# Second transformer block regrouped by tiles 0-1, 2, 3 (early part) and 0-2, 3 (conv FFN), with expert rows spaced wider

## What is computed

```python
# first block
x = x + (sigmoid(gc) * short_conv + sigmoid(ga) * diff_attention) @ w_mix_out
x = x + cross_attention(rmsnorm(x), rmsnorm(mem))
x = x + peer_ffn(rmsnorm(x))          # 8 heads x 16 of 16384 experts per token
x = rmsnorm(x)
# second block
y = concat(rms(nsa_mixer(...)), rms(gmlp_mixer(zg)), rms(conformer_conv(zc, 31 taps)))
x = x + y @ w_out
x = x + memory_cross_attention(x, mem_2)
x = x + conv_ffn(x)                   # up 1024->5632, conv of 3 taps over tokens, silu gate, down 2816->1024
out = rmsnorm(x)
# peer_ffn, per token: act = gelu(h . u_e);  out = sum_e g_e * act * v_e
```

## Time and profile before

| | before |
|---|---|
| median of 3 runs | 2905.69 us (2903.39 to 2906.92) |
| the profiled execution | 2902.87 us, span 2901.1 us, mean granted clock 0.892 |
| TensorE busy | 2408.7 us (83%) |
| VectorE busy | 1765.4 us (61%) |
| ScalarE busy | 1124.4 us (39%) |
| DMA | 838.74 MB, mean 289 GB/s |
| expert gathers (GpSimd queue) | 512, 536.90 MB, first at 557.1 us, last at 2267.5 us |

### The profile page before, as it was taken

The page is one execution under the profiler, slowest core; times in us unless marked ns, Lnnn a source line. Parts: engine busy times, 40 slices in busy tenths (PEclk is TensorE's granted clock), DMA queues, the critical chain, the costliest instruction groups (busy, mean ns, idle before and its releaser), DMA issues.

```text
span 2901.1 us, 31007 instructions
## 1 busy us (share of the span) xinstructions
PE 2408.7 (83%) x10834; PEld 1655.5 (57%) x10834; DVE 1765.4 (61%) x4230; ACT 1124.4 (39%) x2762; POOL 665.2 (23%) x569
## 2 busy tenths in 40 slices
PE   8999999879978649778958588577984799988998
PEld 7786666657744327536626434354762376655873
DVE  2101311598797778676999898888998417312430
ACT  2101311242533764354442578464554225412210
POOL 0000000122343344332233334443234102100000
PEclk9999999989989879999979566699996699999999
DMA  6555343589999999999889989999999653443443
GB/s 205 173 153 166 96 145 126 213 333 371 403 412 417 416 392 391 419 398 393 314 333 416 368 324 379 390 419 419 416 418 419 258 161 111 152 131 94 153 153 116
DMA packets 160972, 838.74 MB, mean 289 GB/s; under 512 B 17400, under 2 KB 21896, under 8 KB 95024
## 3 DMA queue, kind: packets, MB, share of 16 engines
q0 software_dynamic: 73728, 536.90, 45.8%
q1 hardware_dynamic: 82464, 287.75, 28.6%
q10 hardware_dynamic: 4624, 12.11, 1.2%
HBM read 828.27 MB, written 8.41 MB: 288 GB/s over the span
## 4 chain that ended last, share of the span: by engine, by line
PE 50%; DVE 22%; ACT 13%; DMA 10%; issue 4%; POOL 0%; ACTq 0%; DVEq 0%; SPq 0%
PE ps L909 24%; DMA BIG<-in_uv,BIG 9%; DVE BIG L1951 6%; PE ps L929 5%; DVE X L1928 5%; PE ps L930 5%; PE ps L1153 5%; PE ps L910 3%; ACT L1446 2%; PE ps L1180 2%; DVE BIG L1859 1%; DVE BIG L1856 1%; PE ps L1123 1%; PE ps L1102 1%; ACT WK L1228 1%
## 5 line engine op out<-in xcount | busy, mean ns | idle before, releaser
L2168 POOL DMA_INDIRECT BIG<-in_uv,BIG x512 | 622.0, 1215 | 1635.1 <-DVE X L1928 576.0
L909 PE MATMUL ps<-BIG,RING 128*128 128x256 f32 x3472 | 810.6, 386 | 15.2 <-DMA RING<-in_w_cq 4.9
L909 PEld LDWEIGHTS ps<-BIG,RING 128*128 128x128 f32 x3472 | 665.5, 193 | 148.0 <-issue 26.5
L1951 DVE CUSTOM_DVE_ANT_0 BIG<-BIG 128x1024 f32<-128x1024 f32 x512 | 619.2, 1217 | 87.1 <-DMA BIG<-in_uv,BIG 84.8
L1928 DVE SCALAR_TENSOR_TENSOR X<-BIG,small,X 128x1024 f32<-128x1024 f32 x333 | 426.3, 1280 | 75.0 <-ACT small L1450 74.3
L1446 ACT ACTIVATE small<-small 128x1 f32<-128x1 f32 x512 | 102.7, 201 | 640.5 <-DVE small L1951 636.3
L909 PE MATMUL ps<-WK,RING 128*128 128x256 f32 x1232 | 291.0, 389 | 21.3 <-DVE BIG L1707 19.3
L909 PEld LDWEIGHTS ps<-WK,RING 128*128 128x128 f32 x1232 | 238.6, 195 | 62.2 <-DVE BIG L1707 26.8
L929 PE MATMUL ps<-RING,BIG 128*128 128x512 f32 (+1 forms) x448 | 225.7, 585 | 5.6 <-DVE BIG L1686 2.4
L930 PE MATMUL ps<-RING,BIG 128*128 128x512 f32 (+1 forms) x448 | 223.5, 580 | 0.0
L1279 ACT ACTIVATE BIG<-ps 128x256 f32<-128x256 f32 (+2 forms) x143 | 56.5, 397 | 375.8 <-PE ps L910 316.7
(11 more groups left out here) (258 smaller groups left out, 2860.1 us busy)
## 6 DMA issues: line engine op xcount, KB each, us to landing
RING<-in_w_up SPq DMA_DIRECT2D x88, 512.0 KB
RING<-in_w_down SPq DMA_DIRECT2D x66, 512.0 KB
RING<-in_w_pq SPq DMA_DIRECT2D x32, 512.0 KB
RING<-in_w_cc SPq DMA_DIRECT2D x16, 512.0 KB
RING<-in_w_cx SPq DMA_DIRECT2D x16, 512.0 KB
RING<-in_w_cb SPq DMA_DIRECT2D x16, 512.0 KB
RING<-in_w_cv SPq DMA_DIRECT2D x16, 512.0 KB
RING<-in_w_gc SPq DMA_DIRECT2D x16, 512.0 KB
```

The costliest lines, as they stand in the source:

```text
L909: e.matmul(ps[:, 0:256], W[:, j, :], src[:, j, 0:256], start=j == 0, stop=False)
L1951: e.tensor_tensor_reduce(out=u, in0=HF[:, t % 2, :], in1=u, scale=1.0, scalar=0.0, op0=ALU.mult, op1=ALU.add, accum_out=dots[:, k % 8:k % ...
L2168: e.indirect_dma_start(out=slot[i], out_offset=None, in_=I["uv"], in_offset=bass.IndirectOffsetOnAxis(ap=IDX[:, t, c:c + 1], axis=0)).then ...
```

## The change

- The second block's early part (`second(g)`, up to `xo`) runs for three groups, tiles 0-1, tile 2 and tile 3 (`EARLY`), its conv FFN (`ffn(f)`) for tiles 0-2 and tile 3 (`LATE`).
- `work` now has `second(0)`, then, once `total(2)` is placed and all choices are made, `second(1)` (tile 2) and `ffn(0)` (tiles 0-2, `up` with 384 columns a chunk). The part after the weave (`end`) is `second(2)` and `ffn(1)` for tile 3, with `late_down` for three tiles (66 chunks) beside, then `down` of tile 3.
- `beside` takes two or three chunks after each attention step, 8 at `y`, 6 in the norm ahead of `xq`, one after each cross attention step, and the rest in the norm ahead of `up`.
- A `proj_T` chunk costs the planner 1.7 per tile. An expert costs 3.1, 3.1, 3.2, 3.4 for tiles 0 to 3.
- Seven slots from the scores of half 1 to the end (slot 7 holds part of the FFN's activations). `UPT`, the buffers of the up half, are two for tiles 0-2 and four for tile 3.
- Tables, loads and loops are indexed by group; `final_in`, the layer-norm row and the compressed values are loaded once per group, and the eight attention units of tile 2 are scaled on ScalarE, where those of tiles 2-3 had one of two wide scalings on GpSimd (line 2147).

```diff
+EARLY = ((0, 1), (2,), (3,))
+LATE = ((0, 1, 2), (3,))
+def tiles_of(name, h):
+    if name in EARLY_SITES or name in ("mix2", "y", "fa"):
+        return EARLY[h]
+    if name in ("up", "ffn2", "fb", "down"):
+        return LATE[h]
+    return (2 * h, 2 * h + 1) if h < 2 else (0, 1)
...
-        if i >= (8 if self.lent_from is None or (3, 3) in self.chosen else 7):
+        if i >= (8 if self.lent_from is None else 7):
...
-                yield 3.4, "proj_T", site, h, c, m, k
+                yield 1.7 * len(tiles_of(site, h)), "proj_T", site, h, c, m, k
...
+        n = 2 if layer == 1 else len(EARLY[h])
+        for step in self.phase(True, ((4.0, "cross", layer, h, i, lean) for i in range(4 * n + 4))):
+            yield step
+            yield from beside(1)
...
-        for i in range(2):
+        for i in LATE[0]:
             for f in range(22):
                 k = self.next_ring()
                 yield (0, "chunk", "down", f, k), (1.7, "down", 0, f, k, (i,))
...
-        for step in self.phase(True, ((8.0, "nsa", h, i) for i in range(20))):
+        for step in self.phase(True, ((8.0, "nsa", h, i) for i in range(8 * nt + 4))):
...
-            yield from beside(1 + step[3] % 2)
+            yield from beside(2 + step[3] % 2)
...
+    def ffn(self, f, lean, beside=lambda n: ()):
+        yield 0, "mark", ("f", f)
+        yield from self.norm_steps(("ffn2", f), lean)
+        yield from beside(100)
+        for k in range(8):
+            yield (3.0 if k == 7 else 0), "trans", ("ffn2", f), k, lean
+        self.norming = False
+        yield 0, "mark", ("up", f)
+        for step in self.proj_T("up", f, 11, lean):
+            yield step
+            if f and step[1:] == ("out_T", "up", f, 1, 3, lean):
+                yield from self.last(0)
...
+        yield from self.second(2, False, beside)
+        yield from self.ffn(1, False, beside)
+        for f in range(22):
+            k = self.next_ring()
+            yield 0, "chunk", "down", f, k
+            yield 3.4, "down", 1, f, k, (0,)
+        yield 0, "mark", ("out", 1)
+        yield from self.last(1)
...
         yield from self.second(0, True)
+        while ("total", 2) not in self.reached or (3, 3) not in self.chosen:
+            self.light = True
+            yield "wait"
+        self.light = False
+        yield from self.second(1, True)
+        yield from self.ffn(0, True)
         self.light = True
...
-                yield (3.1 if t < 2 else 2.5), "pace"
+                yield (3.1, 3.1, 3.2, 3.4)[t], "pace"
...
-        yield from (s[1:] for s in self.second(1, False))
+        yield from (s[1:] for s in self.end())
...
+                n = 128 * len(tiles_of(site, h))
                 for j in range(7):
-                    e.matmul(ps[:, 0:256], W[:, j, :], src[:, j, 0:256], start=j == 0, stop=False)
+                    e.matmul(ps[:, 0:n], W[:, j, :], src[:, j, 0:n], start=j == 0, stop=False)
...
-                if h == 1 and 0 <= u < 16:
+                if h == 2 and 0 <= u < len(nsa_units(h)):
```

More of the change, by code:

```diff
@@ L325, in late_down, with second @@
         yield (0, "mark", ("out", 0)),
[L327 to L332, removed]
+    def second(self, h, lean, beside=lambda n: ()):
+        nt = len(EARLY[h])
         yield 0, "mark", ("s2", h)
@@ L376, in second @@
         yield 0, "y_scale", h
-        yield from beside(7)
+        yield from beside(8)
         for k in range(8):
@@ L381, in second @@
         yield from self.proj_tok("ou", h, 2, lean)
[L382 to L395, removed]
+        yield from self.cross(2, h, lean, beside)
+    def ffn(self, f, lean, beside=lambda n: ()):
+        yield 0, "mark", ("f", f)
+        yield from self.norm_steps(("ffn2", f), lean)
+        yield from beside(100)
+        for k in range(8):
+            yield (3.0 if k == 7 else 0), "trans", ("ffn2", f), k, lean
+        self.norming = False
+        yield 0, "mark", ("up", f)
[3 more added lines that the diff above has]
+                yield from self.last(0)
     def last(self, h):
@@ L400, in last, with end, beside @@
         yield 0, "store", h
+    def end(self):
+        rest = self.late_down()
+        def beside(n):
+            for steps in islice(rest, n):
+                yield from steps
+        yield from self.second(2, False, beside)
[6 more added lines that the diff above has]
+        yield from self.last(1)
     def first_a(self):
@@ L464, in peers @@
                     yield 0, "total", t - 1
-                yield (3.1 if t < 2 else 2.5), "pace"
+                    self.reached.add(("total", t - 1))
+                yield (3.1, 3.1, 3.2, 3.4)[t], "pace"
             if t % 2:
@@ L611, in program @@
[L611 to L619 removed]
+        L = [L0, L0, SLOT0 + 8448]
@@ new lines, in program, with early @@
+        NT = [len(g) for g in EARLY]
+        def early(first, *shape):
+            return [at_(o + first * n, *[128 * n if d == "w" else n if d == "n" else d for d in shape]) for o, n in zip(L, NT)]
+        QN = early(0, 4, "w")
+        ZG = early(512, "n", 512)
+        CV = early(1024, 2, "w")
+        ZT = early(1280, 2, "w")
+        Y = early(1536, "n", 1024)
+        HTz = early(1536, 8, "w")
+        YT = early(0, 8, "w")
+        HTx = early(2048, 8, "w")
+        QT2 = early(0, 8, "w")
@@ L1411, in cross @@
                             w.wait_ge(*at["mm", "xv", layer, h, hd, d])
-                            e.activation(OT[:, 2 * hd + d, :], banks[ps_of["xv", layer, h, hd, d]][:, 0:256], ACT.Copy,
+                            e.activation(OT[:, 2 * hd + d, :], banks[ps_of["xv", layer, h, hd, d]][:, 0:128 * nt], ACT.Copy,
                                          scale=1.0).then_inc(act.sem, act("ev", "xv", layer, h, hd, d))
@@ L2161, in expert @@
                     w.wait_ge(*at["sum", slot_before[k]])
-                    if i == NS - 1 and slot_before[k] == plan.lent_from:
-                        w.wait_ge(*at["idx", 3, 3])
                 else:
@@ L2200, in gpsimd_program @@
                             channel_multiplier=-1).then_inc(pool.sem, pool("ws"))
-            follow({"norm_out": norm_out, "nsa": nsa, "out_T": out_T, "expert": expert, "mark": marks(pool, "pool")})
+            follow({"nsa": nsa, "out_T": out_T, "expert": expert, "mark": marks(pool, "pool")})
         for engine_program in (tensor_program, vector_program, scalar_program, gpsimd_program, sync_program):
```

341 lines of the change are left out of this document (183 added, 158 removed).

## The result

| | before | after |
|---|---|---|
| median | 2905.62 us (2899.99 to 2914.76) | 2913.01 us (2906.92 to 2915.69) |
| ratio | | 1.0023, 95% interval 1.0016 to 1.003 |
| span of the profiled execution | 2901.1 us | 2910.0 us |
| `second(0)`, to PE's last record of `xo` (1482 to 1991.6; 1479.5 to 1939.1) | 509.6 us, 164 dots | 459.6 us, 130 dots |
| last dot of an expert | 2283 | 2400 |

A forecast was written before the change was run, and what follows sets the result against it. DVE was taken to bound 1482:1823 and DMA the rest to 2283, with PE busy 578 of the tail's 618 us. Last dot at 2365, plus 74 for remaining `up` chunks and 386 of tail, gave 2825, rounded to 2828 us; range 2785 to 2885.

The forecast's parts named there:

- One tile halves: Tail of tile 3: 128 moving columns take about 0.11 us a record, a one-tile weight chunk of 16 records 1.72 us.
- Rival 4: Tail: 128-row weight loads don't run under 128-column multiplies, 0.214 us a record; +110 us, 2938 us; chance 0.03.
- Rival 1: Tail: SP's queue starves the ring at 226 GB/s, 2.32 us a one-tile chunk; +64 us, 2892 us; chance 0.10.
- Rival 2: Weave: seven slots instead of eight allow only 3.93 us an expert; +106 us, 2934 us; chance 0.08.
- Rival 3: Weave: the plan's unit costs 1.25 us, not the expert; last dot at 2538, about 3000 us; chance 0.07, mostly in part.
- Rival 5: Weave: better balance, DVE and DMA reach 94%, last dot near 2330; 2790 us; chance 0.10.
- sign of being wrong: The prediction is wrong if the experts' last dot comes after 2440 or the tail exceeds 450 us.
- 33.5 for 42 saves 8.7 x 2.58: Norm, projections and compression of tiles 0-1: 33.5 experts instead of 42 at 2.58 us each save 22 us of 148.
- 45 for 58 in the DMA-bound stage saves 12.6 x 2.51: `ou` to `xo` of tiles 0-1: 45 experts instead of 58 at 2.51 us of DMA each save 32 us of 175.
- my step to 432 for the totals by DVE and by bytes: Tile 2's experts: stages sum to 440 us; totals give 434 by DVE, 424 by bytes; 432 was taken.
- PE can be some five chunks ahead: After the last expert: 19 `up` chunks of three tiles remain, but PE's lead leaves 14 or 15, 74 us.
- `last(0)` in it costs about 10 us of DVE and ScalarE, which eight banks cover: `up` of tile 3: `last(0)` hides under eight banks (13.8 us); without that cover it costs up to 10 us.

The follow-up runs named there:

- e1: Changed kernel with only the store of tiles 0-2's output placed 12 chunks later in `up` of tile 3; 2896.98 us, 0.9968 of before.
- e3: Changed kernel with the eighth slot given back to the experts after the last choice; 2915.14 us, 1.0028 of before.
- e2: Changed kernel with the old expert spacing of 2.5 units for tiles 2 and 3, so regrouping alone; 2999.77 us, 1.0319 of before.
- e5: Changed kernel with the store 12 chunks later and tile 3's experts at 4.8 units ahead of `up`, 3.4 beside it; 2853.65 us, 0.9817 of before.

## Why the prediction was wrong

**Right.** The plan's stages: `second(0)` took all of tile 2's experts, tile 3's ended after 24 chunks of `up` (forecast 25), some 20 were left (19), and a chunk of 384 columns took 5.16 us (5.13). The tail without its stall: 391 us in e1 for 386. One tile halves: 128 records of 128 columns ran in 14.5 us (2765.9 to 2780.4), 0.113 us each, where I had 0.107 to 0.11. The norm, projections and compression of tile 2 took 97.4 us for 92, and its `y` to `up` 121.8 for 121, with DMA full in both. Rival 4 is out. The sentence of the Trainium skill that stood beside it (TensorE: Matmul & The Clock Gate, The mechanism; I had named the section behind it), by which weight loads overlap multiplies in flight only when they use other row groups, does not hold for this shape. The same section also has loads pulled ahead when they go to the background weight buffer; whether that is what happened, no run here shows. Rival 1 is out: the ring gave a one-tile `up` chunk every 1.79 us, PE's own pace. Rival 2 is out by e3. Rival 3 was wrong in size, 1.09 us a unit and not 1.25, but right that the work beside has a cost of its own. Rival 5 (last dot near 2330) is out too. Neither sign of being wrong came (last dot after 2440, tail over 450): the miss is four terms of 16 to 27 us that all went the same way.

**The first failed step, +22 and +16: "33.5 for 42 saves 8.7 x 2.58" and its two neighbours.** I priced each expert that leaves a stage at the full time of the resource that looked busiest, 2.5 to 2.6 us (1.8 in the attention), and so took DVE or DMA for a hard bound in every stage. Between PE's marks `second(0)` gave back 50 us for 34.5 experts, 1.45 us each. Worst was "45 for 58 in the DMA-bound stage saves 12.6 x 2.51": `y` to `xo` gave back 4 us for 9 experts, and at the changed kernel's density neither half the bytes (0 us) nor the shorter sums (0.5 us) made it shorter; PE is busy 127 us of its 148. The share of 1.01 in the earlier trace rows did not make the DMA the bound there. Norm to compression gave 2.1 us an expert and not 2.58. The attention gave more than I took, 28 us for 22, because 17 experts left it and not 12. The cuts of the earlier trace rows, put where the plan has its stages, lay up to 17 us beside PE's (its attention ended at 1840 and not 1823, its `up` ran from 2011 to 2196 and not from 1998 to 2208), which hid this. My three terms came to 76 us, to 440; the remaining 8 us of the +22 are my step to 432 for the totals by DVE and by bytes, which price in the same way.

The forecast for the early part of tile 2, 310 us, was a sum of each stage's largest resource at full use. Up to `up` it took 340: +12 ahead of the attention (6 of them `xo` of tiles 0-1, still running), +13 in the attention (115 us for 102, DVE busy 99 of them and the DMA share 0.75), +1 behind it, and +6 for the six ring buffers whose lead I had taken off. The experts' part of `up` then took 127 for 141, which leaves the +16.

**The second, +27: "PE can be some five chunks ahead".** That took the state of 1998:2208, where PE waited, over to a stage where PE bounds: beside the 35 experts PE did its 24 to 25 chunks of 5.16 us without a pause and was never ahead. My own two terms, 141 + 74 = 215 us for all 44 chunks, lay below the 44 x 5.13 = 226 that PE needs. Adding them up would have shown it. (That 1.5 x 3.45 is 5.18 and not 5.13 adds 2 us at most.) The gap of those two terms is 12 us of the 27; the other 15 are only the last dot coming earlier in `up` than forecast, and stand with the other sign in the 127 for 141.

**The third, +23: "`last(0)` in it costs about 10 us of DVE and ScalarE, which eight banks cover".** The cover was right for these two engines. Missing was the store at the end of `last(0)`: I had written that SP's ring order follows PE's, and had not counted the one other instruction that `last` puts on that queue. It cost 18.3 us of the 23 in the traces (97.2 against 78.9 for `up`) and 16 in the medians; the few left are spread over the tail.

**What the change is worth.** The tail became 208.5 us shorter. What lies ahead of it became 220 us longer: tile 2's early part and the norm behind it are 334 us that were not there, `up` takes 42 us more (227 for 185), and against that stand 50 us less in `second(0)`, 19 us for the norm ahead of `up` of tiles 0-1 (now counted with tile 2's) and the 87 us in which experts had run alone. It pays by the number of experts that lie beside the 227 us of `up`, where PE is the bound and each is free: with none (e2) it costs 94 us, with 35 it comes out nearly even, and with 61 and the later store (e5) the kernel is 1.8% faster than before and 2.0% faster than the changed one.

**Open.** What the 707 us are made of in detail is argued from PE's waits, not shown: no run took a norm's chain out of the queues, or the other half of the bytes and the dots. Whether DVE or DMA sets the limit of some 61 experts beside `up` is open too. Nor was it tried to take the rows ahead of a residual out of DVE's order alone.

## What to carry to other kernels

Price a move by what the stage gives back for one unit less, read from two stretches or two kernels with different density (here 0.5 to 2.1 us by stage, and 1.8 in tile 2's early part, not the 2.5 of the busiest resource), with the stretches cut at the engine's own records and not where the plan has them. Then put the filler beside the stage that another engine fills to 100%. Where two terms of a sum describe one stage, add them and hold them against that stage's own engine. When a group of steps is moved, list what each puts on every queue: here a store that waited for a result kept the loads behind it out for 20 us, and the ring of six lasted 10.7 us (6 x 1.79).

## What the runs showed of the hardware

After the 15.38 us in which PE stood still, its first 14 records of 128 columns took 3.33 us, the same 14 before 1.73: it came back at half the clock (1.2 for 2.4 GHz). In the 6.6 us behind the stall the granted clock was 0.53, and then 1.00 again:

```profile
2795.80:2802.40 6.60, 6.59 (x33) 6.60 (x34) 1.14 (x4) 2.05 (x3) 0.00 (x0) 0.53 0.98 384
2802.40:2863.10 60.70, 60.70 (x546) 60.70 (x545) 38.17 (x135) 18.93 (x51) 7.27 (x16) 1.00 0.85 287
```

That made the stall cost 18.3 us instead of 15.4. In e1, with no such gap, the granted clock was 1.00 over the whole of this `up`. In `up` of tiles 0-2 it was 1.00 for 227 us on end, beside the experts too, where the two stretches before it had 0.73 and 0.72: here the stage that PE fills is also the one in which PE is fastest.

A DMA share of 1.01 at 413 GB/s stood over a stage that hardly became shorter with fewer bytes (`y` to `xo`, 152 us before and 148 after), and one of 1.02 at 418 GB/s over a stage that did (tile 2's `y` to `up`, 122 us, with half the bytes 106): the share alone does not tell whether the DMA bounds.
